# Four modulation tiles summed as columns in the front, x transposed before its modulation, two more tiles moved into the first mixer

## The reference

```
cond = silu(c)
for l in range(2):
    mod = cond @ ada_w[l] + ada_b[l]                      # 6 x 1024 values
    sh1, sc1, g1, sh2, sc2, g2 = split(mod, 6)
    h = rms_norm(x, norm1_g[l]) * (1 + sc1) + sh1
    z, xbc, dt, mq, mk, mv, sq, sk, sv = split(h @ w_in[l])
    y = concat(ssd_mixer(z, xbc, dt), moba_attention(mq, mk, mv), swa_attention(sq, sk, sv)) @ w_out[l]
    x = x + g1 * y
    h = rms_norm(x, norm2_g[l]) * (1 + sc2) + sh2
    x = x + g2 * peer_ffn(h)                              # top-16 of 128^2 experts, 8 heads
```

## Time and profile before

| | |
|---|---|
| median of 3 runs | 3392.22 us (3388.09 to 3393.9) |
| the profiled execution | 3391.35 us, its span 3389.6 us |
| TensorE (PE) busy | 3297.0 us, 97% of the span |
| VectorE (DVE) busy | 2483.4 us, 73% |
| ScalarE (ACT) busy | 1574.6 us, 46% |
| GpSimd (POOL) busy | 106.2 us, 3% |
| moved by DMA | 689.63 MB, mean 203 GB/s |

### The profile page before, as it was taken

One profiled execution on the slowest core, in us unless ns is written; L12 is line 12 of the kernel. 1 busy time (PEld: TensorE's weight loads), 2 busy tenths in 40 slices (PEclk: granted clock), 3 DMA queues, 4 the chain that ended last, 5 costly groups with the idle time before them and its releaser, 6 DMA issues.

```text
span 3389.6 us, 50635 instructions
## 1 busy us (share of the span) xinstructions
PE 3297.0 (97%) x19934; PEld 2913.5 (86%) x19934; DVE 2483.4 (73%) x4335; ACT 1574.6 (46%) x1883; POOL 106.2 (3%) x32
## 2 busy tenths in 40 slices
PE   7999999999999999999999999999999999999999
PEld 4889999888888899998888878888888888888887
DVE  7879996777887769986667777566667675655575
ACT  4544454333335544544443344463454454544553
POOL 0014000000000041000000000000000000000000
PEclk9999999999999999999999999999999999999999
DMA  9454567778874344566667775543445555434453
GB/s 379 175 184 178 196 224 265 272 281 284 285 278 157 110 174 176 212 239 219 222 212 238 245 260 188 197 150 125 162 164 186 189 193 198 158 126 149 153 193 141
DMA packets 172164, 689.63 MB, mean 203 GB/s; under 512 B 12396, under 2 KB 78724, under 8 KB 99223
## 3 DMA queue, kind: packets, MB, share of 16 engines
q1 hardware_dynamic: 167492, 663.86, 54.8%
q10 hardware_dynamic: 4436, 22.53, 1.8%
HBM read 650.66 MB, written 35.68 MB: 202 GB/s over the span
## 4 chain that ended last, share of the span: by engine, by line
PE 90%; DVE 4%; ACT 2%; PEld 1%; issue 1%; DVEq 1%; DMA 1%; PEldq 0%; ACTq 0%
PE ps L1243 20%; PE ps L853 15%; PE ps L905 12%; PE ps L956 8%; PE ps L859 7%; PE ps L911 7%; PE ps L963 3%; PE ps L1204 3%; PE ps L875 3%; PE ps L881 1%; PE ps L988 1%; ACT weights_upper L1510 1%; PE ps L900 1%; DVE weights_lower L2017 1%; PE ps L925 1%
## 5 line engine op out<-in xcount | busy, mean ns | idle before, releaser
L1510 ACT ACTIVATE weights_upper<-weights 128x2048 fp32r<-128x2048 f32 x520 | 996.2, 1917 | 1515.1 <-issue 510.3
L2017 DVE TENSOR_TENSOR weights_lower<-weights,weights_upper 128x2048 fp32r<-128x2048 f32 x498 | 1142.0, 2295 | 506.9 <-ACT weights_upper L1510 506.4
L853 PE MATMUL ps<-hT_span,weights_upper 128*128 128x256 f32 x4352 | 548.4, 284 | 0.0
L853 PEld LDWEIGHTS ps<-hT_span,weights_upper 128*128 128x128 f32 x4352 | 531.8, 192 | 4.8 <-issue 3.5
L905 PE MATMUL ps<-hT_span,weights_upper 128*128 128x512 f32 x1664 | 397.3, 391 | 0.0
L905 PEld LDWEIGHTS ps<-hT_span,weights_upper 128*128 128x128 f32 x1664 | 305.8, 188 | 59.2
L859 PE MATMUL ps<-hT_span,weights_lower 128*128 128x256 f32 x2240 | 291.6, 283 | 0.0
L859 PEld LDWEIGHTS ps<-hT_span,weights_lower 128*128 128x128 f32 x2240 | 278.9, 192 | 0.0
L1243 PE MATMUL ps<-weights_upper,hidden_lower 128*128 128x512 f32 x1008 | 250.7, 391 | 0.0
L1243 PE MATMUL ps<-weights_upper,hidden_upper 128*128 128x512 f32 x1008 | 249.0, 389 | 0.0
L1243 PE MATMUL ps<-weights_lower,hidden_upper 128*128 128x512 f32 x1008 | 248.9, 389 | 0.0
(11 more groups left out here) (412 smaller groups left out, 3985.0 us busy)
## 6 DMA issues: line engine op xcount, KB each, us to landing
weights<-in_parts SPq DMA_DIRECT2D x264, 1024.0 KB, 4.8
weights<-in_experts SPq DMA_DIRECT2D x256, 1024.0 KB, 4.9
scr<-gates SPq DMA_DIRECT2D x32, 1024.0 KB, 8.4
work<-in_ada_s SPq DMA_DIRECT2D x96, 256.0 KB, 5.3
gates<-h SPq DMA_DIRECT2D x16, 1024.0 KB, 4.8
gates<-work SPq DMA_DIRECT2D x16, 1024.0 KB, 4.8
weights<-in_ada_w SPq DMA_DIRECT2D x6, 2048.0 KB, 15.2
scr<-in_ada_l SPq DMA_DIRECT2D x35, 256.0 KB, 6.3
```

The costliest lines, as they stand in the source:

```text
L853: m = mm(bank[:, e * T:(e + 1) * T], up[:, c, e * P:(e + 1) * P], src[1 - n][:, c, :], start=(e == 0 and n == 0 and c == 0), stop=False, s ...
L1510: f(upper[:, p_.r % SPLIT, :], raw[:, p_.r, :], ACT.Copy).then_inc(upper_ready, 1)
L2017: v.tensor_tensor(lower[:, s, :], raw[:, p_.r, :], upper[:, s, :].bitcast(F32), ALU.subtract)\
```

## The change

- Four tiles in place of six are summed in the front, in the order 2, 0, 3, 1 (scale and shift of the first half of the columns, then of the second), from ring slot 0 on. The tiles 8 and 9 join `ADA_BACK`, which has eight tiles and so 64 pieces.
- VectorE sums five chunks of a front tile, TensorE three. TensorE now has the tile as the stationary side, in blocks of 128 columns, and two columns as the moving side: 12 products and 4 sums of 128 x 2 a tile. The values stand as columns on the partitions, where the features of the transposed tokens are.
- x is not modulated before it is transposed. VectorE makes a diagonal of 1/deviation for each half of the tokens, and TensorE multiplies x by it (`scaled_transposes`) behind the second tile. ACT applies scale and shift on the way out of PSUM (`modulated`), once rounded as the upper half and once whole; VectorE subtracts for the lower half (`lower_halves`) and makes the columns of gain and shift (`front_columns`).
- Bias and gain of the first norm come in one load of 128 x 24, `front_col`, behind x on ACT's queue; the two bias rows and the gain row are no longer loaded. VectorE waits for it ahead of its first tile.
- SP issues tile n once tile n - 2 has landed; ahead of the fourth tile it waits until TensorE has used the first, and loads the first raw part before it.
- VectorE's pieces stand as 5 for 4 in the four places of `xbc`, 5 for 3 ahead of `sq` (two places) and `z`, 6 for 5 and 7 for 2 in `wout`; behind the second norm 16 are left, as before. The second norm reads its shift from PSUM, in halves.

```diff
-ADA_DVE = 6
+ADA_DVE = 5
...
-ADA_FRONT = (8, 9, 2, 0, 3, 1)
-ADA_BACK = (4, 5, 6, 7, 10, 11)
+ADA_FRONT = (2, 0, 3, 1)
+ADA_BACK = (4, 5, 8, 9, 6, 7, 10, 11)
...
-FIRST_SLOT = 2
+FIRST_SLOT = 0
...
             for (name, i), n in firsts[0].tiles.items():
                 sp.sem_inc(S("held"), 1)
+                if n >= 2:
+                    sp.wait_ge(*k.landed("ada", n - 2))
+                    sp.sem_inc(S("held"), 1)
+                if n == len(ADA_FRONT) - 1:
+                    sp.wait_ge(*k.slot_over(0))
+                    e = part(firsts[0], 0, "xbc", 0)
+                    sp.wait_ge(*e.raw_free())
+                    sp.dma_start(raw[:, e.r, :], a["parts1"][0, 0]).then_inc(raw_landed[e.r], 16)
                 load(k, name, i, a["ada_w"][n])
...
                     for c in range(ADA_DVE, KC):
-                        mm(k.bank("ada", i), cT[:, c:c + 1].broadcast_to([P, P]), w[:, c, :], start=(c == ADA_DVE),
-                           stop=False)
...
-                    mm(k.bank("ada", i), ones[0:1, :], ada_bias(c_), start=False, stop=False)
-                    if i == len(ADA_FRONT) - 1:
-                        transposes(k, "hT", h, "h1_half", 0, banks=(0, 1))
+                        for b_ in range(4):
+                            mm(k.bank("ada", i)[:, 2 * b_:2 * b_ + 2], w[:, c, b_ * P:(b_ + 1) * P], cT_next[:, c:c + 2],
+                               start=(c == ADA_DVE and b_ == 0), stop=False, skip_group_check=True)
                     pe.wait_ge(S("ada_acc"), i + 1)
-                    mm(k.bank("ada", i), ones, mod[:, c_ * NBLK:(c_ + 1) * NBLK], start=False, stop=True)\
-                        .then_inc(k.fill_sem("ada", i), 1)
+                    for b_ in range(4):
+                        m = mm(k.bank("ada", i)[:, 2 * b_:2 * b_ + 2], scr[:, c_ * NBLK + b_ * P:][:, 0:P], ones[:, 0:2],
+                               start=False, stop=True, skip_group_check=True)
+                    m.then_inc(k.fill_sem("ada", i), 1)
                     pe.drain().then_inc(k.used_sem("ada", i), 1)
-                if l == 0:
-                    transposes(k, "hT", h, "h1", 0, banks=(2, 3))
...
+                    if i == 1:
+                        scaled_transposes(k, "hT", 0, signal="x_diag")
...
             act.dma_start(x[:, :, :], a["x"][0].rearrange("(a p) n -> p a n", a=TT)).then_inc(S("x_in"), 16)
+            act.dma_start(stat(328, 24), a["front_col"]).then_inc(S("front_col_in"), 16)
...
+                def modulated(half):
+
+
+                    act.wait_ge(S("front_cols"), half + 1)
+                    for i in (2 * half, 2 * half + 1):
+                        act.wait_ge(*k.filled("hT", i))
+                        act.sem_inc(S("held"), 1)
+                        for whole in range(2):
+                            for c in (2 * i, 2 * i + 1):
+                                m = f(h_all[:, c * T:(c + 1) * T] if whole else hT_up[:, c, :],
+                                      k.bank("hT", i)[:, (c % 2) * T:(c % 2 + 1) * T], ACT.Identity,
+                                      scale=gain_col[:, c:c + 1], bias=shift_col[:, c:c + 1])
+                            m.then_inc(S("whole1" if whole else "upper1"), 1)
...
+                def front_columns(half):
+
+
+                    c = slice(4 * half, 4 * half + 4)
+                    scale, shift = (k.bank("ada", 2 * half + j)[:, 0:8].rearrange("p (b e) -> p b e", e=2)[:, :, 0]
+                                    for j in range(2))
+                    v.wait_ge(*k.filled("ada", 2 * half))
+                    v.tensor_tensor(gain_col[:, c], scale, scale_bias[:, c], ALU.add)\
+                        .then_inc(k.empty_sem("ada", 2 * half), 1)
...
                 for i, c_ in enumerate(ADA_FRONT if l == 0 else ()):
-                    if i == len(ADA_FRONT) - 1:
-                        modulated(0)
+                    if i == 0:
+                        v.wait_ge(S("front_col_in"), 16)
+                        v.tensor_scalar(scale_bias, scale_bias, 1.0, None, ALU.add)
                     v.wait_ge(*k.landed("ada", i))
...
+                    elif i == 2:
+                        front_columns(0)
+                        lower_halves(0)
...
                 for i in range(4):
-                    late_pieces(4 * i, 4)
+                    late_pieces(5 * i, 5)
                     ahead("xbc", i)
...
-                for j in range(2, 4 if l == 0 else 2):
-                    v.wait_ge(*k.emptied("late", j))
-                scaled_and_shifted(gain2, mod[:, 3 * D:4 * D], 2 * l * TT, "h2")
+                if l == 0:
+                    for j in (4, 5):
+                        v.wait_ge(*k.filled("late", j))
+                    v.sem_inc(S("held"), 1)
+                    scaled_and_shifted(gain2, [k.bank("late", j) for j in (4, 5)], 0, "h2")
```

137 lines of the change are left out of this document (69 added, 68 removed).

## The result

| | before | changed |
|---|---|---|
| median of 16 runs | 3392.14 us (3388.09 to 3396.91) | 3400.94 us (3398.19 to 3408.66) |
| the profiled execution, its span | 3391.35, 3389.6 | 3398.59, 3396.6 |

The ratio is 1.0027, 95% interval 1.002 to 1.0035. Forecast were 3401.4, in a range from 3390 to 3408. Every ratio here compares fast executions; two slow ones, of 11511 us (the kernel before) and of 4088 us (the last run with GpSimd), are left out of them.

What follows compares the result with a forecast made beforehand. TensorE, busy 97% of the span, was taken as the bound. 1.0 - 1.1 + 3.3 + 3.3 - 0.7 + 4.1 - 1.4 + 0.4 + 0.3 = +9.2 on 3391.35, plus 0.9: 3401.4; range 3390 to 3408.

Steps and rivals of the forecast that it cites:

- x and VectorE's start: Start of the front: x lands at 22.5, and VectorE, waiting for the column load behind it, starts at 22.8.
- The front's steps: Front, from first sum at 28.8 to second lower part done at 60.7, before 59.7: +1.0.
- What TensorE's first lower pass waits for: End of the front: TensorE's first lower pass begins right behind VectorE's second lower weight part, 59.68 and 59.92 before.
- The price of a narrow pair: TensorE's front products: a pair costs 0.11 at the full clock or 0.213 at the half clock, whatever it moves.
- xbc: The four products of xbc: four more pieces on VectorE, +3.3, less 1.1 of its wait for a piece.
- Up to z: From the front through the query and key tiles: VectorE's whole push reaches TensorE at 126.37, 5.8.
- The hidden pieces: Two pieces ahead of z and one ahead of wout's second lower part: hidden by idle time, otherwise 1.6 and 0.8.
- wout and the second norm: Behind wout's second lower part: seven pieces for two, +4.1, waits gone, -1.4, second norm's shift in halves, +0.4.
- Rival 1: Front: narrow pairs near 0.11, or TensorE holds its full clock; fourth tile 8.9 earlier, sum +0.3, 3392.5; chance 28%.
- Rival 2: Front: the column load does not wait for x; fourth tile 6.6 earlier, sum +2.6, 3394.8; chance 8%.
- Rival 3: Front: the clock never lifts; fourth tile ends at 57.0, +4.1 more, sum +13.3, 3405.5; chance 14%.
- Rival 4: Mixer at 125.54: VectorE's added pieces are off the path; with rival 1's front the sum is -7.2, 3385; chance 5%.

Runs made afterwards that it cites:

- the last run with GpSimd: Changed kernel with the column load first, all eight chunks of front tiles on VectorE, and 16 pieces of tiles 8 and 9 on GpSimd: 3412.80 us, ratio 1.0062.
- the reordered front: Changed kernel, column load first, eight chunks on VectorE, third tile ahead of the diagonals, first half's lower halves behind the fourth tile: 3387.38 us, ratio 0.9991.
- the run without six pieces: Changed kernel where VectorE leaves out six pieces of wout, one ahead of the second lower part and five behind it: one run, 3403.28 us.
- leaving out the 16 pieces: Changed kernel where VectorE leaves out 16 of the 64 late pieces, in xbc, sq, z and wout, with loads and waits kept: 3395.39 us, ratio 1.0012.

## Why the prediction was right, point by point

The time (3401.4 forecast, 3400.9 measured) and the mechanism, VectorE's added pieces at the places where TensorE follows it, were right. That the two times lie 0.5 apart is partly luck: several terms were right only in the sum of parts that were not.

- **x and VectorE's start.** Forecast 22.5 and 22.8. x was there at 19.8. The forecast had carried the constants' landing over from the kernel before (13.49) and let x follow 9.0 later; the constants landed some 5.5 earlier, at about 8.0, and x 11.8 behind them, the same 11.8 as before. The 12 KB load landed at 23.0 all the same, 20.9 us after its issue and 3.2 after x. Issued first, it took 2.5 us. That it waits behind the queue was right, but not that it lands as soon as x does, and the 0.2 of agreement is luck.
- **The front's steps.** First sum 28.8 (28.8 measured), second sum 36.0 (36.0), transposes 41.9 (42.0), third tile 45.9 (45.5), fourth 52.9 (51.5), column work to 53.4 (51.6), second lower part done 60.7 (59.7). The term was +1.0 and came out at 0.0: the clock fell in the middle of the fourth tile (4.02) and not ahead of it (5.25), and from the columns to the end of the lower part it took 8.1 and not 7.3. Of the seven other profiles with this form of tile, two show 5.25 and five 3.93 to 4.34, and where the front has no edit at all it ended from 0.0 to 2.9 over that of before.
- **What TensorE's first lower pass waits for** was misread. The earlier trace rows has L859 at 59.92 right behind the second lower part (59.68), and the forecast took the one for the cause of the other. In the changed kernel L864 starts at 58.34 and the second lower part is done at 59.7; with the reordered front it is 44.94 and 46.9. The path through VectorE held all the same, since its queue from there on has next to no idle time.
- **The price of a narrow pair** was right at both ends: 24 pairs take 2.74 (0.114) and 5.25 (0.219). By the rule of the Trainium skill ("TensorE: Matmul & The Clock Gate", section "LDWEIGHTS (loading the stationary operand)") a weight load takes about 107 ns. With the 25 ns that the section "Wait — 56ns, not 53.3ns?" of the same page gives as the least distance of two matmuls, the pair was an estimated 0.132 at either clock. The trace has 0.114 where TensorE runs fast, near the load alone, and 0.219 where it runs slow; its weight loads are recorded at 0.192 and 0.333. So the load goes with the clock, and the measurement decides.
- **xbc.** +3.3 for the pieces and -1.1 for the wait; the wait gave 1.66, so 1.7 in all and not 2.2.
- **Up to z.** 5.8 forecast, 5.4 measured, out of other parts: VectorE brings only 4.3 (126.37's L1061 has its like at 131.3, and the first of the pair comes 4.29 later, at 129.46). The other 1.1 is TensorE's clock, a term that I had only behind the second norm: new idle time of 3.10 ahead of the segment sums, and their two pairs take 1.19 and 1.06 where they took 0.67.
- **The hidden pieces.** Right: VectorE is 5.97 late at the z parts and 5.43 in wout, so the two ahead of z and the one ahead of the second lower part cost nothing.
- **wout and the second norm.** +4.1 - 1.4 + 0.4 = 3.1 forecast, 3.46 measured between the lower parts. The term was mis-sized as a reason: the run without six pieces shows that five of them are worth only 1.9 there, since the gain waits for ACT's copy of the tiles 8 and 9. I had the change of that wait in the diff (four late tiles in place of two) and gave it no price. The halves out of PSUM take 1.41 for 1.28, twice.
- **TensorE's idle time at the second norm** was to be about 7 and is 4.52: the added sum of two late tiles (L1037) stands in it and pushes the four products (L795) behind it.
- **Rival 1** (narrow products quick in the front) fell: they are quick only where wide work has just lifted the clock. Its price was also summed wrong: by its own terms the fourth tile would be there at 43.3, 9.6 earlier, and not at 44.0. **Rival 2** (the column load does not wait) fell, and its price was about right: with that load first, the front came 5.2 earlier (6.6 said), less because the constants and x then land later, x by 3.5. **Rival 3** (the clock never lifts) is what single executions come near: 5.25 for the fourth tile. **Rival 4** (slack at 125.54) fell: L1063 starts right behind L2248.

What stays open: how the front's clock falls is different from execution to execution, and how much of the 10 us between the changed kernel's fastest and slowest run this is was not measured. Nor is it measured why leaving out the 16 pieces brings the time down by half of the 8.8 only, where its wq mark comes down by 6.8.

## What to carry to other kernels

Work that is moved off the start must be paid where it goes: here leaving two tiles out of the front is worth 8 us in its old form (12.8 with the new form, the column load first and VectorE's reordering together), and they cost 6 to 11 in the mixer, because the engine that takes them is the one that the mixer waits for. Read the queue ahead of an early load by its order and not by its size, put a tiny load that an engine waits for first, but watch what it does to the loads behind it (x came 3.5 us later), and look for what is queued behind a waiting instruction (10 us lay in one such order on VectorE). When added work hides an older wait, taking the work away gives only the difference: leave it out once, on the chip, before pricing it.
